# Two FFN products in one 512-column matmul, and half of each low part on GpSimd, in a float32 transformer kernel

## What is computed

```python
def conv_ffn(h, w_up, conv_w, conv_b, w_down):        # first block; conv over tokens -1, 0, +1
    u = h @ w_up                                      # [tokens, 2 * 2816]
    acc = conv_b
    for j in range(3):
        acc = acc + pad(u)[:, j:j + L] * conv_w[j]
    a, g = split(acc, 2)
    return (silu(g) * a) @ w_down
def conv_ffn_2(x, w_in, conv_w, conv_b, w_out):       # second block; conv over tokens -2, -1, 0
    ...
```

## Time and profile before

| what | value |
|---|---|
| median of three runs | 1633.01 us (1632.73 to 1633.6) |
| span of the profiled execution | 1629.6 us |
| PE busy, of that span | 1587.4 us (97%) |
| DVE, ACT, POOL busy | 1047.1, 809.9, 236.8 us |
| chunks of `up1`, `fin0` and `fin1` | 3 x 22 |

### The profile page before, as it was taken

The page is one execution under the profiler, slowest core; times in us unless marked ns, Lnnn a source line. Parts: engine busy times, 40 slices in busy tenths (PEclk is TensorE's granted clock), DMA queues, the critical chain, the costliest instruction groups (busy, mean ns, idle before and its releaser), DMA issues.

```text
span 1629.6 us, 27020 instructions
## 1 busy us (share of the span) xinstructions
PE 1587.4 (97%) x10876; PEld 1372.2 (84%) x10876; DVE 1047.1 (64%) x1952; ACT 809.9 (50%) x1537; POOL 236.8 (15%) x282
## 2 busy tenths in 40 slices
PE   7999999999999999999999999999999999999998
PEld 4788778877777888887899988878999898799986
DVE  3734856465345434787787767766777667767765
ACT  2414963432233323567455554655555566555553
POOL 0202320011010100012011101142111013311110
PEclk9999999999999999999999999999999999999999
DMA  9765022354564323021455453334555543345552
GB/s 365 290 247 208 24 77 103 155 207 155 207 232 181 103 97 136 27 79 53 164 185 212 169 201 124 131 105 155 182 181 182 197 140 123 133 146 187 182 194 78
DMA packets 39852, 257.29 MB, mean 158 GB/s; under 512 B 5552, under 2 KB 6832, under 8 KB 11056
## 3 DMA queue, kind: packets, MB, share of 16 engines
q1 hardware_dynamic: 36848, 249.61, 42.1%
q0 software_dynamic: 1296, 4.72, 0.8%
q10 hardware_dynamic: 1584, 1.23, 0.3%
HBM read 254.49 MB, written 1.05 MB: 157 GB/s over the span
## 4 chain that ended last, share of the span: by engine, by line
PE 85%; DVE 9%; ACT 4%; issue 1%; DMA 1%; ACTq 0%; POOL 0%; DVEq 0%; SPq 0%
PE ps L486 25%; PE ps L488 25%; PE ps L487 25%; PE ps L502 3%; PE ps L634 1%; PE ps L656 1%; PE ps L643 1%; DVE ps L2101 1%; PE ps L1109 1%; DVE wl L1848 1%; PE ps L528 1%; DMA raw<-in_ada 1%; PE ps L615 1%; ACT wh L1374 1%; ACT arena L1445 1%
## 5 line engine op out<-in xcount | busy, mean ns | idle before, releaser
L1842 DVE TENSOR_TENSOR wl<-raw,wh 128x1024 fp32r<-128x1024 f32 (+3 forms) x318 | 371.1, 1208 | 346.1 <-ACT wh L1374 345.5
L1374 ACT CAST wh<-raw 128x1024 fp32r<-128x1024 f32 (+2 forms) x328 | 322.7, 1033 | 489.0 <-PE ps L488 399.2
L486 PE MATMUL ps<-xh,wh 128*128 128x256 f32 (+1 forms) x1582 | 493.6, 312 | 3.7 <-DVE wl L1848 3.2
L488 PE MATMUL ps<-xh,wl 128*128 128x256 f32 (+1 forms) x1582 | 488.6, 309 | 0.0
L487 PE MATMUL ps<-xl,wh 128*128 128x256 f32 (+1 forms) x1582 | 488.5, 309 | 0.0
L486 PEld LDWEIGHTS ps<-xh,wh 128*128 128x128 f32 x1582 | 301.8, 191 | 28.9 <-issue 9.3
L487 PEld LDWEIGHTS ps<-xl,wh 128*128 128x128 f32 x1582 | 302.0, 191 | 15.1 <-issue 0.7
L488 PEld LDWEIGHTS ps<-xh,wl 128*128 128x128 f32 x1582 | 301.9, 191 | 15.2
L486 PE MATMUL ps<-wh,xh 128*128 128x512 f32 (+3 forms) x812 | 298.6, 368 | 2.0 <-issue 0.8
L488 PE MATMUL ps<-wh,xl 128*128 128x512 f32 (+3 forms) x812 | 293.2, 361 | 0.0
L487 PE MATMUL ps<-wl,xh 128*128 128x512 f32 (+3 forms) x812 | 293.1, 361 | 0.0
(11 more groups left out here) (215 smaller groups left out, 1835.4 us busy)
## 6 DMA issues: line engine op xcount, KB each, us to landing
raw<-in_ada SPq DMA_DIRECT2D x48, 1024.0 KB, 6.2
raw<-in_up SPq DMA_DIRECT2D x44, 1024.0 KB, 5.4
raw<-in_fin SPq DMA_DIRECT2D x44, 1024.0 KB, 4.8
raw<-in_down SPq DMA_DIRECT2D x22, 1024.0 KB, 4.8
raw<-in_fout SPq DMA_DIRECT2D x22, 1024.0 KB, 4.8
raw<-in_win SPq DMA_DIRECT2D x12, 1024.0 KB, 4.9
raw<-in_ev_w_in SPq DMA_DIRECT2D x9, 1024.0 KB, 7.2
raw<-in_wout SPq DMA_DIRECT2D x8, 1024.0 KB, 4.8
```

What stands on the lines that cost most here:

```text
L486: e.matmul(out, A[0], B[0], start=first, stop=False)
L488: return e.matmul(out, A[1], B[0], start=False, stop=last)
L1374: e.copy(hi_of(j)[:, a:b], raw_of(j)[:, a:b]).then_inc(*S.hi.up((j, half)))
L1842: e.tensor_tensor(lo_of(j)[:, a:b], raw_of(j)[:, a:b], hi_of(j)[:, a:b].bitcast(F), ALU.subtract).then_inc(*S.lo.up((j, half)))
```

## The change

In the FFNs of 256 tokens the two products with the high weights become one matmul of 512 columns. The high and low parts of the tokens are placed in one tile `xx`, and `hidden_beside` takes both as the moving operand: columns 0 to 255 of the bank hold high weights times high tokens, columns 256 to 511 high times low plus low times high. The two half banks must then be added: ACT copies the second half to SBUF, and DVE adds the first half to it. The middle tap and the other taps read this sum from SBUF in place of PSUM. Silu of chunk f - 1 moves ahead of the middle taps of chunk f on ACT. The first half of the low part of chunks 2 to 21 is made by GpSimd, ahead of its product of the chunk, and the second half stays on DVE.

```diff
-    xh = sb("xh", [128, 8, 512], R)
-    xl = sb("xl", [128, 8, 512], R)
+    xx = sb("xx", [128, 2, 8, 512], R)
+    xh, xl = xx[:, 0, :, :], xx[:, 1, :, :]
...
+    FIRST_ON_POOL = {J[up, f] for up in ("up1", "fin0", "fin1") for f in range(2, NT)}
...
         def wait_chunk(j):
             q.wait_ge(*S.hi.at((j, 1)))
+            q.wait_ge(*low_done(j, 0))
             q.wait_ge(*low_done(j))
...
+        def hidden_beside(up, f, part, ks=range(8)):
...
+            both = ps[b][:, :].rearrange("p (s n) -> p s n", s=2)
+            for k in ks:
+                if k < 7:
+                    e.matmul(both, hv[:, k, fs], xx[:, :, k, 0:256], start=k == 0, stop=False)
+                m = e.matmul(both[:, 1, :], lv[:, k, fs], xh[:, k, 0:256], start=False, stop=False)
+                if k == 7:
+                    m = e.matmul(both, hv[:, k, fs], xx[:, :, k, 0:256], start=False, stop=True)
...
 # ACT
                 weights(after(J[up, f]))
+                for part in range(2) if ngrp == 1 else ():
+                    q.wait_ge(*S.proj.at((up, f, part)))
...
+                    e.copy(temp(up, f)[:, part, 256:512], ps[2 * (f % 3) + part][:, 256:512]).then_inc(
+                        *S.act.up(("rest", up, f, part)))
+                if f and ngrp == 1:
+                    gate(f - 1)
                 for part in range(2):
...
+                    if ngrp == 1:
+                        q.wait_ge(*S.vec.at(("whole", up, f, part)))
+                        src = temp(up, f)[:, part, 256:512]
...
-                    e.activation(temp(up, f)[:, part, 0:n], ps[2 * (f % 3) + part][:, 0:n], ACT.Identity,
+                    e.activation(temp(up, f)[:, part, 0:n], src, ACT.Identity,
                                  bias=w[3], scale=w[1 if up[0] == "u" else 2]).then_inc(*S.act.up(("tap", up, f, part)))
-                if f:
+                if f and ngrp == 2:
                     gate(f - 1)
...
 # DVE
-            for half, a, b in halves(j):
+            for half, a, b in halves(j)[1 if j in FIRST_ON_POOL else 0:]:
...
                 weights(after(J[up, f]))
+                for part in range(2) if ngrp == 1 else ():
+                    rest = temp(up, f)[:, part, 256:512]
+                    q.wait_ge(*S.act.at(("rest", up, f, part)))
+                    e.tensor_tensor(rest, ps[2 * (f % 3) + part][:, 0:256], rest, ALU.add).then_inc(
+                        *S.vec.up(("whole", up, f, part)))
...
-                    src = ps[2 * (f % 3) + part][:, 0:n].rearrange("p (g t) -> p g t", g=ngrp)
+                    src = ps[2 * (f % 3) + part][:, 0:n] if ngrp == 2 else temp(up, f)[:, part, 256:512]
+                    src = src.rearrange("p (g t) -> p g t", g=ngrp)
...
 # POOL
-            for half, a, b in halves(j):
+            for half, a, b in halves(j)[0:1 if j in FIRST_ON_POOL else 2]:
...
                 beside(f)
+                if after(J[up, f]) in FIRST_ON_POOL:
+                    weights(after(J[up, f]))
                 q.wait_ge(*S.act.at(("silu", up, f)))
                 t = temp(up, f)
                 e.tensor_tensor(ACTF[:, f, 0:n], t[:, 1, 0:n], t[:, 0, 0:n], ALU.mult).then_inc(*S.prod.up((up, f)))
...
 # SP, before it fills the buffer of chunk j - NRAW again
                     q.wait_ge(*S.hi.at((j - NRAW, 1)))
+                    q.wait_ge(*low_done(j - NRAW, 0))
                     q.wait_ge(*low_done(j - NRAW))
```

More of the change, by code:

```diff
@@ L276, in low_done @@
     def low_done(j, half=1):
-        return (S.lop if j in ON_POOL else S.lo).at((j, half))
+        return (S.lop if j in ON_POOL or half == 0 and j in FIRST_ON_POOL else S.lo).at((j, half))
     def hi_of(j):
@@ L719, in hidden @@
             return m
+        def hidden_beside(up, f, part, ks=range(8)):
+            j, b = J[up, f], 2 * (f % 3) + part
+            hv, lv = (v.rearrange("p (k n) -> p k n", k=8) for v in (hi_of(j), lo_of(j)))
+            fs = slice(128 * part, 128 * part + 128)
+            both = ps[b][:, :].rearrange("p (s n) -> p s n", s=2)
[5 more added lines that the diff above has]
+                    m = e.matmul(both, hv[:, k, fs], xx[:, :, k, 0:256], start=False, stop=True)
+            return m
         def hidden_free(up, f):
             for part in range(2):
-                free[2 * (f % 3) + part] = [(S.conv, (up, f, part))]
+                free[2 * (f % 3) + part] = [(S.conv, (up, f, part)) if up == "up0" else (S.vec, ("whole", up, f, part))]
         def by_features(up, key, g):
@@ L733, in by_features @@
                 for part in range(2):
-                    m = hidden(up, 0, part, g, 256, [k])
+                    m = hidden(up, 0, part, g, 256, [k]) if up == "up0" else hidden_beside(up, 0, part, [k])
             return m
@@ L754, in ffn @@
                     wait_bank(2 * (f % 3) + part)
-                    hidden(up, f, part, 0, 256 * ngrp).then_inc(*S.proj.up((up, f, part), ("use", J[up, f])))
+                    m = hidden(up, f, part, 0, 512) if ngrp == 2 else hidden_beside(up, f, part)
+                    m.then_inc(*S.proj.up((up, f, part), ("use", J[up, f])))
                 hidden_free(up, f)
@@ L1547, in ffn @@
                 weights(after(J[up, f]))
+                for part in range(2) if ngrp == 1 else ():
+                    q.wait_ge(*S.proj.at((up, f, part)))
+                    for signal, at in wait(f):
+                        q.wait_ge(*signal.at(at))
+                    e.copy(temp(up, f)[:, part, 256:512], ps[2 * (f % 3) + part][:, 256:512]).then_inc(
+                        *S.act.up(("rest", up, f, part)))
+                if f and ngrp == 1:
+                    gate(f - 1)
                 for part in range(2):
                     w = [conv(i, f + NT * part) for i in range(4)]
-                    q.wait_ge(*S.proj.at((up, f, part)))
                     if f >= 2:
                         q.wait_ge(*S.prod.at((up, f - 2)))
-                    for signal, at in wait(f):
-                        q.wait_ge(*signal.at(at))
-                    e.activation(temp(up, f)[:, part, 0:n], ps[2 * (f % 3) + part][:, 0:n], ACT.Identity,
+                    if ngrp == 1:
+                        q.wait_ge(*S.vec.at(("whole", up, f, part)))
+                        src = temp(up, f)[:, part, 256:512]
+                    else:
+                        q.wait_ge(*S.proj.at((up, f, part)))
+                        for signal, at in wait(f):
+                            q.wait_ge(*signal.at(at))
+                        src = ps[2 * (f % 3) + part][:, :]
+                    e.activation(temp(up, f)[:, part, 0:n], src, ACT.Identity,
                                  bias=w[3], scale=w[1 if up[0] == "u" else 2]).then_inc(*S.act.up(("tap", up, f, part)))
-                if f:
+                if f and ngrp == 2:
                     gate(f - 1)
@@ L2179, in ffn @@
                 weights(after(J[up, f]))
+                for part in range(2) if ngrp == 1 else ():
[3 more added lines that the diff above has]
+                        *S.vec.up(("whole", up, f, part)))
+                    if part:
+                        q.wait_ge(*S.vec.last())
                 for part in range(2):
                     acc = temp(up, f)[:, part, 0:n].rearrange("p (g t) -> p g t", g=ngrp)
-                    src = ps[2 * (f % 3) + part][:, 0:n].rearrange("p (g t) -> p g t", g=ngrp)
+                    src = ps[2 * (f % 3) + part][:, 0:n] if ngrp == 2 else temp(up, f)[:, part, 256:512]
+                    src = src.rearrange("p (g t) -> p g t", g=ngrp)
                     q.wait_ge(*S.act.at(("tap", up, f, part)))
@@ L2661, in weights @@
         def weights(j):
-            if j is None or j not in ON_POOL:
+            if j is None or j not in ON_POOL and j not in FIRST_ON_POOL:
                 return
-            for half, a, b in halves(j):
+            for half, a, b in halves(j)[0:1 if j in FIRST_ON_POOL else 2]:
                 q.wait_ge(*S.hi.at((j, half)))
```

## The result

| kernel | median of the runs | span of the profiled execution |
|---|---|---|
| before | 1633.3 us (1632.73 to 1633.67, 4 runs) | 1629.6 us |
| changed | 1670.56 us (1669.28 to 1673.54, 4 runs) | 1668.8 us |

The ratio is 1.0231, with a 95% interval of 1.0217 to 1.0246. The change costs 37 us where 27 were forecast. The time lies within the range of 1645 to 1677 us, though above the 1655 to 1667 of the forecast itself. The span grew by 39.2 us and the median by 37.3: a run's time stands 1.2 to 1.6 us above its own span wherever both are recorded, so the 1629.6 is the span of one of the quicker runs of the kernel before.

A forecast was written before the change was run, and what follows sets the result against it. PE bounds the kernel before; afterwards DVE and POOL excluding each other at 6.2 us per chunk. 10.4 for `up1` plus 2 x 8.6 for `fin0` and `fin1` makes 27.6 us, so about 1660 us; range 1645 to 1677.

The forecast's parts named there:

- r: Zero point in each FFN chunk: the moment ACT starts casting chunk f + 2, released by PE's last matmul of chunk f.
- the ring: FFN first halves: POOL's low half and product, DVE's low half and four taps exclude each other; taken as 6.2 us per chunk.
- The strict reading of the rule: DVE and POOL in FFN chunks: shared port pair locked for each whole instruction, making the ring an estimated 6.4 us.
- The lateness of chunk 3: `up1`: chunk 3 first late, 1.0 for order of work plus 1.28 for Silu's table load, 2.1 us after what is given back.
- Then 18 chunks at 6.2 in place of 5.76: `up1`: the following 18 chunks run at the slower pace, costing 7.9 us.
- the splits: Activation splits at f = 6 and 10, on DVE 0.69 us each with two SBUF inputs; 1.0 us taken in all.
- The clock: Whole kernel: PE busy 90% of each chunk would keep its granted clock of 1.00, so priced at nothing.
- another pace than 226.7 ns: FFN first halves: sign that the forecast is wrong, if the 512-column matmul on two runs doesn't take 226.7 ns.
- the order alone counts: FFNs: only POOL's order counts, taps slip past POOL without waiting; pace 6.05 us, 1651 us; chance 0.18.
- The ring at full length: FFNs: mutual exclusion of DVE and POOL takes 6.4 us or above per chunk, 1673 us; chance 0.19.
- POOL's half is in time: FFNs: chunk f + 2 ready at r + 5.3, PE unbroken, gain 14.1 us, 1619 us; chance 0.08.
- no change: FFNs: chunk f + 2 ready at about r + 5.7, the stall gives back just 0.21 us, 1633 us; chance 0.05.

The follow-up runs named there:

- e2: Kernel before with only POOL's half of the low parts added, matmuls and PSUM taps as before; 1664.02 us, ratio 1.0195.
- e8: Kernel before with POOL's half of the low parts added, placed ahead of POOL's product of the chunk before; 1635.57 us, ratio 1.0018.
- e3: Changed kernel with POOL's low half of chunk f + 3 moved ahead of its product of chunk f; 1694.13 us, ratio 1.0371.
- e12: Changed kernel with POOL's half ahead of its product, the sum in PSUM, and DVE's additions ahead of its low half; 1633.13 us, ratio 1.0006.
- e4: Changed kernel with the sum of the half banks written back to PSUM, so taps read PSUM; POOL's order kept; 1657.72 us, ratio 1.0156.
- e9: Changed kernel with DVE making all low parts, sum in PSUM, additions ahead of second low half, and the 512 moving columns in one run; 1628.05 us.
- e7: Changed kernel with DVE making all low parts, sum in PSUM, and DVE's additions ahead of its second low half; 1626.99 us, ratio 0.9968.
- e6: Changed kernel with DVE making all low parts and the sum of the half banks in PSUM; 1657.43 us, ratio 1.0152.

## Why the prediction was right, and where its terms were off

**The mechanism, as forecast.** POOL's low half stood behind its product, that behind Silu, that behind the casts and copies. It was ready at r + 6.32 where 6.3 was forecast. That these agree to 0.02 us is partly luck: the product started 0.2 us sooner than forecast (2.93, not 3.13) and was held up by as much beside DVE. Two chunks took about 12.3 us where 12.1 was forecast by this chain. e2 shows that this part of the change costs 31 of 37 us, and e8 that in the kernel before the order is what costs. In the changed kernel the order alone could not be mended: with it turned round (e3) the other ring took over, 24 us slower, and the loss went only when DVE's order was changed too (e12). That DVE's order alone would mend the changed kernel, with POOL's left as it is, was not run.

**The exclusion of DVE and POOL, as forecast, but not where it was put.** The first tap took over 2 us beside POOL's half (2.63 for the first two, of which the second takes 0.52). In `fin`, where the forecast took the ring at 6.2 as the bound, the steady pace was 6.17, but e4 has 6.15 without the taps' part: the chain through POOL's order bound. The ring ran nearly level with it: DVE's round from 1245.94 to 1251.98 took 6.04 us with no gap but the 0.47 in which it waits for ACT. The strict reading of the rule, 6.4, didn't hold in `fin`. DVE instructions with one input in PSUM go on beside POOL (four taps in 2.04 us, e4), and those with two in SBUF don't (4.09 us, e3). The Trainium skill, "SBUF — State Buffer", section "SBUF: two separate sides", says the same: a DVE instruction takes the shared lock if it has two SBUF inputs, against a GpSimd one that reads SBUF. The traces agree.

**The terms of the sum.** For `fin0` and `fin1` 8.6 us each were forecast, and they took 8.2 and 7.8. For `up1` 10.4 were forecast, and it took 15.6. The lateness of chunk 3 was right (chunk 2 took 7.93 us, 2.2 more than 5.76; 2.1 was forecast). The step that was off is "Then 18 chunks at 6.2 in place of 5.76": with the splits these chunks were to cost 8.9 us, and they cost 13.8. In chunks 5 to 12 the pace was 6.5 and more. DVE and POOL there, in the changed kernel:

```profile
838.67 0.69 DVE L2096 TENSOR_TENSOR X<-arena 128x512 f32<-128x512 f32 x1
839.28 1.77 DVE L1874 TENSOR_TENSOR wl<-raw,wh 128x1024 fp32r<-128x1024 f32 x1
...
842.18 2.96 DVE L2226 SCALAR_TENSOR_TENSOR arena<-arena,pv 128x255 f32<-128x255 f32 x4 [0.47 <-ACT arena L1587]
...
839.23 0.74 POOL L2753 TENSOR_TENSOR arena<-arena 128x256 f32<-128x256 f32 x1 [2.44 <-ACT arena L1559]
839.92 3.39 POOL L2706 TENSOR_TENSOR wl<-raw,wh 128x1024 fp32r<-128x1024 f32 x1
```

The row work has two SBUF inputs and joins the ring. POOL's product slips in ahead of DVE's low half, and then POOL's half is the one that waits (3.39). I had read one chunk near 890 us, behind the end of the row work, and took it for all of `up1`; the same instructions stand in the kernel before, at 843.12 for one. Around 887 POOL's program also issues two DMAs ahead of a low half, 1.15 us which the forecast left out; that chunk took 7.41 us:

```profile
887.06 1.15 POOL L2720 DMA_DIRECT2D arena<-in_ln_rows  x2
888.22 2.37 POOL L2706 TENSOR_TENSOR wl<-raw,wh 128x1024 fp32r<-128x1024 f32 x1
```

And near the end of `up1` the side task's matmul waits for ACT's copy, which stands behind the middle taps, which wait for the additions behind a DVE low half of 3.44 us beside POOL's; that chunk took 9.74 us, against 6.61 in the kernel before (PE, DVE):

```profile
930.81 1.10 PE L619 MATMUL ps<-tmp,cs 128*128 128x512 f32 x2 [2.77 <-ACT arena L1442]
...
925.24 3.44 DVE L1874 TENSOR_TENSOR wl<-raw,wh 128x1024 fp32r<-128x1024 f32 x1
```

**What was priced at nothing.** The second halves start with ACT and DVE behind. In `fout0` PE waits for an activation split, which it doesn't in the kernel before:

```profile
1287.21 0.47 PE L490 MATMUL ps<-wh,xx 128*128 128x512 f32 x1 [1.82 <-DVE xx L2199]
```

From the start of `fout0` to that of `fin1` the changed kernel takes 192.0 us and the one before 188.2, from that of `fout1` to the end 68.0 against 66.7. That is 5 us of the 10 that were missing. The first halves make 4 more, and 0.8 lies from the start of `down1` to that of `fin0`. The clock, also priced at nothing, was right: its granted share was 1.00 in all three first halves.

**The matmuls.** 5.55 us per chunk was forecast and 5.64 is what the pairs take, 0.12 less than 5.76 and not 0.21. The prediction had named another pace than 226.7 ns as a sign of being wrong: a pair takes 352 and not 346.7 ns, but the two runs of the moving operand, which it had in doubt, aren't the reason (e9). The full gain of the merging is so 7.9 us and not 14.1 (e7 reaches 7.6 of it in its three first halves, which are 2.1, 2.8 and 2.7 us shorter, and 5.7 of it in the whole). With widths together it is 0.17 per chunk. By the Trainium skill, "TensorE: Matmul & The Clock Gate", section "Wait — 56ns, not 53.3ns?", 2.6 us were estimated. The measured 7.9 lies between that and the 14.1 of the forecast, and the measurement decides.

**The rivals.** That the order alone counts (1651) is what bound in `fin`, but its condition, that the taps slip past POOL, is refuted by the 2.63 us of two taps, and its time is 20 us short. The ring at full length (1673) comes nearest in time, 2 us off, and for another reason than it gave: `fin` ran at 6.17 and not 6.4, and the loss beyond the forecast came from the row work, the DMAs and the side task in `up1` and from the second halves. So it is in part luck that the range, which was made wide enough for this rival, holds the time. That POOL's half is in time (1619), or late by little enough for no change (1633), is refuted by its end at r + 6.32.

## What to carry to other kernels

Work that is moved to an idle engine lands in that engine's order: what its next instruction waits for now stands ahead of it, and here it was the end of a chain of three engines. Before moving, write out which instructions of the two engines have two SBUF inputs; where these exclude each other, the share that one gives away comes back as waiting, and an instruction of 0.69 us can take 2.85. Where an engine waits for another in every round, put the next piece of ready work into the gap (e7). Here that was worth 30 us, and the share given to GpSimd was worth nothing at best.

## What the runs showed that I had not expected

Matmuls of 512 and 256 columns in turn take 352 ns per pair, though the two widths by themselves take 226.7 and 120.0; grouped by width and weights' tile, a chunk fell from 5.64 to 5.59 us. Two runs of 256 moving columns and one of 512 cost the same. And e6 ran for twelve chunks of `fin0` and `fin1` at 5.64 us and from then on at 6.10, with the same program. The step came with the activation split at f = 10 (0.69 us on DVE): before it POOL's product started during DVE's second low half and waited, after it the product fell between the two. With an engine that has no slack, one extra instruction set the pace for the rest of the stage.
